# Gate and up products of two transformer layers by Strassen's scheme

## The reference

```
h2 = rmsnorm(x, norm_ffn[l])
gu = einsum('btd,df->btf', h2, w_gate_up[l])      # 1024 x 5632
g, up = split(gu, 2)
x = x + einsum('btf,fd->btd', silu(g) * up, w_down[l])   # 2816 x 1024
```

## Time and profile before

| | |
|---|---|
| median of 3 runs | 2195.66 us (2195.58 to 2195.78) |
| profiled execution | 2195.95 us |
| its span | 2194.1 us |
| busy in the span | PE 2182.2, weight loads 1812.8, DVE 1377.9, ACT 965.4, POOL 74.7 us |
| granted TensorE clock | 0.999 of 2.4 GHz, mean |

### The profile page before, as it was taken

How to read it: one execution, slowest core, us unless ns; L and a number is a source line. 1 busy time by engine, 2 the same in 40 slices (tenths; PEclk the granted TensorE clock), 3 DMA queues, 4 the chain that set the end, 5 groups by cost and what they waited for, 6 DMA issues and landing times.

```text
span 2194.1 us, 28930 instructions
## 1 busy us (share of the span) xinstructions
PE 2182.2 (99%) x10528; PEld 1812.8 (83%) x10528; DVE 1377.9 (63%) x1978; ACT 965.4 (44%) x1392; POOL 74.7 (3%) x103
## 2 busy tenths in 40 slices
PE   9999999999999999999999999999999999999998
PEld 6878888888888878888888888888888899888887
DVE  7999954444345999954444334654776568888723
ACT  5678544443223588544343223332554344333412
POOL 0000020000010000020000010000000000000000
PEclk9999999999999999999999999999999999999999
DMA  5221222222223211222222224223222231222222
GB/s 184 73 80 63 96 96 96 96 96 84 93 93 119 93 62 63 95 96 97 97 99 94 83 92 150 100 81 127 81 97 87 96 135 39 101 99 99 93 96 77
DMA packets 35397, 208.39 MB, mean 95 GB/s; under 512 B 4512, under 2 KB 5024, under 8 KB 14816
## 3 DMA queue, kind: packets, MB, share of 16 engines
q1 hardware_dynamic: 35296, 207.07, 27.2%
HBM read 201.15 MB, written 2.10 MB: 93 GB/s over the span
## 4 chain that ended last, share of the span: by engine, by line
PE 94%; ACT 3%; DVE 2%; issue 1%; DMA 0%; SPq 0%; DVEq 0%; ACTq 0%
PE mm L1796 25%; PE mm L1798 25%; PE mm L1797 25%; PE sp L1798 4%; PE sp L1797 4%; PE sp L1796 4%; PE sp L1898 1%; PE ob L1926 1%; ACT probs L584 1%; DVE conv_y L1171 1%; DVE probs L1201 1%; ACT probs L592 1%; PE sp L1913 0%; PE ob L1798 0%; PE ob L1796 0%
## 5 line engine op out<-in xcount | busy, mean ns | idle before, releaser
L1796 PE MATMUL mm<-in_hi,w_hi 128*128 128x512 f32 (+1 forms) x1696 | 663.6, 391 | 2.9 <-DVE in_lo L1104 2.3
L1798 PE MATMUL mm<-in_hi,w_lo 128*128 128x512 f32 (+1 forms) x1696 | 657.0, 387 | 0.0
L1797 PE MATMUL mm<-in_lo,w_hi 128*128 128x512 f32 (+1 forms) x1696 | 656.9, 387 | 0.0
L525 ACT ACTIVATE w_hi<-w_raw 128x2048 fp32r<-128x2048 f32 (+3 forms) x193 | 346.1, 1794 | 672.7 <-PE mm L1798 562.2
L1070 DVE TENSOR_TENSOR w_lo<-w_raw,w_hi 128x2048 fp32r<-128x2048 f32 (+3 forms) x193 | 422.2, 2188 | 238.7 <-ACT w_hi L525 238.3
L1796 PEld LDWEIGHTS mm<-in_hi,w_hi 128*128 128x128 f32 x1696 | 318.4, 188 | 74.2 <-issue 6.7
L1798 PEld LDWEIGHTS mm<-in_hi,w_lo 128*128 128x128 f32 x1696 | 318.4, 188 | 65.5
L1797 PEld LDWEIGHTS mm<-in_lo,w_hi 128*128 128x128 f32 x1696 | 318.5, 188 | 64.2 <-issue 1.0
L1171 DVE SCALAR_TENSOR_TENSOR conv_y<-conv_in,parl,conv_y 128x512 f32<-128x512 f32 x240 | 169.8, 746 | 1.7
L1081 DVE TENSOR_TENSOR tB<-mm,rstd 128x512 f32<-128x512 f32 x54 | 37.3, 690 | 172.6 <-PE mm L1798 172.6
L1796 PE MATMUL mm<-act_hi,w_hi 128*128 128x512 f32 x352 | 136.9, 389 | 0.0
(11 more groups left out here) (429 smaller groups left out, 3252.9 us busy)
## 6 DMA issues: line engine op xcount, KB each, us to landing
w_raw<-in_w_dram SPq DMA_DIRECT2D x160, 1024.0 KB, 4.8
w_raw<-in_w_dram SPq DMA_DIRECT2D x32, 704.0 KB, 3.9
w_raw<-in_w_dram SPq DMA_DIRECT2D x5, 512.0 KB, 4.5
out_dram<-z_rows SPq DMA_DIRECT2D x8, 256.0 KB, 2.1
rope<-in_rope_dram SPq DMA_DIRECT2D x3, 512.0 KB, 3.9
x<-in_x_dram SPq DMA_DIRECT2D x4, 256.0 KB, 4.9
x<-in_x_dram SPq DMA_DIRECT2D x2, 512.0 KB, 7.6
sq<-ssum SPq DMA_DIRECT2D x32, 32.0 KB, 1.8
```

Source lines behind the costliest of these rows:

```text
L525: e.activation(whi[:, slot, 0:cols], raw[:, slot, 0:cols], ACT.Copy).then_inc(s_whi, whi_out.up())
L1796: MM(out, ah, bh, start=first, stop=False, **kw)
L1797: MM(out, ah, bl, start=False, stop=False, **kw)
L1798: return MM(out, al, bh, start=False, stop=last, **kw)
```

## The change

The gate and up weights of a pair of tiles are seen as a 2 x 2 matrix of blocks: A11 and A12 are the gate tile's first and second four k-tiles, A21 and A22 the up tile's. The tokens are one too: B11, B12, B21, B22, by the first and second four k-tiles and by the first and second 256 tokens. Instead of eight block products, seven are made (Winograd's form of Strassen's scheme), each 4 k-tiles x 3 passes of 256 columns:

- weights: S1 = A21 + A22, S2 = A11 - S1 (the code's wsum 2), S3 = A21 - A11 (wsum 4), S4 = A12 + S2. S1 and wsum 4 are made on POOL (`weight_sums`), the other two on DVE.
- tokens: T1, T2, T3, T4 from differences and sums of the B, made once in a layer by DVE during the output projection.
- products, in TensorE's order for pair p: S1 T1, then A22 T4 of pair p - 1, S2 T2, A12 B21, A11 B11 of pair p + 1, S3 T3, S4 B22. Sums of products are made in PSUM where they can be; three partial results are copied out by ACT (`copied`) and added by DVE (`take_product`).

So the high and low parts of the weights are made in seven pieces of 512 columns (`high_of`, `low_of`), and a raw slot is free once the low part of A22 is made (`load_free`). The chain per pair on DVE is written out in `gated_pair`. The high and low part of the first 12 `act` tiles (`KEPT`) are made only when the stage is over, and the down product takes its k-tiles in the order 12 to 21, 0 to 11 (`DOWN_ORDER`).

The core of the diff, in this order: SP, POOL (`weight_sums`), ACT (to the first `gated_pair`), DVE (to the second), TensorE:

```diff
-L_MM = 102
+L_MM = 58
+KEPT = 12
+DOWN_ORDER = tuple(range(KEPT, FT)) + tuple(range(KEPT))
...
+            def load_free(n, slot, read, cols=CH):
+                e.wait_ge(s_so, read)
+                e.dma_start(raw[:, slot, 0:cols],
+                            W[bass.ds(n, 1), :, 0:cols].rearrange("a p c -> (a p) c")).then_inc(s_raw[slot], 16)
...
+                with L.loop(0, L_GU // 2 - 1) as i:
+                    for c in range(2):
+                        load_free(n + (gate_up + 2) + i * 2 + c, c, operands.now(-8))
+                        operands.skip(7)
...
+                def weight_sums(a, fifth_done):
+                    e.wait_ge(s_raw[a], raws[a].next(16))
+                    e.wait_ge(s_sm, done.now(-fifth_done))
+                    e.tensor_tensor(spot(wsum, 1), raw[:, a, A21], raw[:, a, A22], ALU.add).then_inc(s_su, made.up())
+                    e.wait_ge(s_sm, done.now(-6))
+                    e.tensor_tensor(spot(wsum, 4), raw[:, a, A21], raw[:, a, A11],
+                                    ALU.subtract).then_inc(s_su, made.up())
+                    done.skip(7)
...
+                def next_weights(p):
+                    e.wait_ge(s_su, summed.next())
+                    high_of_sum(1)
+                    e.wait_ge(s_ds, sums.next())
+                    high_of_sum(2)
+                    e.wait_ge(s_sm, done.now(-4))
+                    high_of(3, raw[:, (p + 1) % 2, A12])
+                    e.wait_ge(s_ds, sums.next())
+                    high_of_sum(spot_s4(p + 1))
...
+                def weights_beyond(p):
+                    landed(p % 2)
+                    high_of(0, raw[:, p % 2, A11])
...
+                def gated_pair(p, m, split):
+                    silu()
+                    copied(copy_5[p % 2], bank_z[p % 2], 1)
+                    e.wait_ge(s_su, summed.next())
+                    high_of_sum(4)
+                    e.wait_ge(s_sm, done.now(-2))
+                    high_of(6, raw[:, p % 2, A22])
+                    copied(copy_2[p % 2], bank_x[p % 2], 3)
+                    if split:
+                        act_high(m)
+                    if p < FT - 1:
+                        next_weights(p)
+                        copied(copy_1[(p + 1) % 2], bank_x[(p + 1) % 2], 5)
+                        if p < FT - 2:
+                            weights_beyond(p)
...
+                def out_second(m):
+                    k = m - HK
+                    g_k, g = col(parl, A_GF + k), col(parl, A_GF + m)
+                    t2, t3, t4 = (token_operand(SUM, o, k) for o in (T2, T3, T4))
+                    e.wait_ge(s_fn, fn.next())
+                    STT(t2, t2, g_k, tB[:, 0:TH], ALU.mult, ALU.subtract).then_inc(s_val, val.up())
+                    STT(t3, x[:, k, second_half], g_k, tB[:, 0:TH], ALU.mult, ALU.subtract).then_inc(s_val, val.up())
+                    e.wait_ge(s_val, val.now(1))
+                    STT(t4, x[:, m, first_half], g, t2, ALU.mult, ALU.add).then_inc(s_val, val.up())
+                    token_low(B21, k, x[:, m, first_half], g)
+                    token_low(T2, k, t2)
+                    token_low(T3, k, t3)
+                    token_low(T4, k, t4)
+                    token_low(B22, k, x[:, m, second_half], g)
...
+                def sums_for_next(p):
+                    a = (p + 1) % 2
+                    e.wait_ge(s_su, summed.next())
+                    e.wait_ge(s_sm, done.now(-3))
+                    TT(spot(wsum, 2), raw[:, a, A11], spot(wsum, 1), ALU.subtract).then_inc(s_ds, wsums.up())
+                    low_of_sum(1)
+                    e.wait_ge(s_ds, wsums.now())
+                    TT(spot(wsum, spot_s4(p + 1)), raw[:, a, A12], spot(wsum, 2),
+                       ALU.add).then_inc(s_ds, wsums.up())
...
+                def lows_for_next(p):
+                    low_of_sum(2)
+                    low_of(3, raw[:, (p + 1) % 2, A12])
+                    low_of_sum(spot_s4(p + 1))
...
+                def take_product(dst, bank, other, product, copy):
+                    e.wait_ge(s_sm, done.now(-product))
+                    e.wait_ge(s_sc, copies.now(-copy))
+                    TT(dst, bank, other, ALU.add).then_inc(s_sv, products.up())
...
+                def act_of(p, m, product, told):
+                    e.wait_ge(s_sm, done.now(-product))
+                    e.wait_ge(s_do, own.now())
+                    TT(tile(actf, m, 0, TH), bank_x[p % 2], tC[:, 0:TH], ALU.mult).then_inc(s_sv, products.up())
+                    TT(tile(actf, m, TH, T), tB[:, 0:TH], tC[:, TH:T], ALU.mult).then_inc(told.sem, told.up())
...
+                def lower_takes(p, products_at, beyond):
+                    seventh, third = products_at
+                    take_product(tB[:, 0:TH], bank_x[p % 2], copy_5[p % 2], seventh, 2)
+                    if beyond:
+                        low_of(0, raw[:, p % 2, A11])
+                    take_product(tA[:, TH:T], bank_z[p % 2], copy_2[p % 2], third, 3)
+                    scaled_gate()
...
+                def gated_pair(p, m, split):
+                    scaled_silu()
+                    e.wait_ge(s_su, summed.next())
+                    low_of_sum(4)
+                    act_of(p - 1, m, 2, val if split else own)
+                    low_of(6, raw[:, p % 2, A22])
+                    sums_for_next(p)
+                    if split:
+                        act_low(m)
+                    upper_takes(p, 4)
+                    lows_for_next(p)
+                    lower_takes(p, (6, 7), p < FT - 2)
...
+            def times(out, n, o, start, ready=None):
+                for k in range(HK):
+                    if ready is not None:
+                        e.wait_ge(s_cmb, combos.now(-ready(k)))
+                    a = slice(k * P, k * P + P)
+                    ins = mm3(out, spot(whi, n)[:, a], spot(wlo, n)[:, a], token_operand(HIGH, o, k),
+                              token_operand(LOW, o, k), start and k == 0, k == HK - 1, skip_group_check=True)
+                ins.then_inc(s_sm, done.up())
...
+            def gated_pair(p):
+                a = p % 2
+                e.wait_ge(s_sv, products.now(5))
+                operand(2)
+                times(bank_z[a], 1, T1, True)
+                e.wait_ge(s_sv, products.now(2))
+                operand(1)
+                times(bank_x[1 - a], 6, T4, False)
+                e.wait_ge(s_sc, copies.now(-1))
+                operand(3)
+                times(bank_x[a], 2, T2, False)
+                e.wait_ge(s_sv, products.now(3))
+                operand(4)
+                times(bank_y, 3, B21, True)
+                last = p == FT - 1
+                if not last:
+                    e.wait_ge(s_sv, products.now(0))
+                    operand(6)
+                    times(bank_x[1 - a], 0, B11, True)
+                e.wait_ge(s_sc, copies.now(-3))
+                operand(6 if last else 7)
+                times(bank_x[a], 4, T3, False)
+                e.wait_ge(s_sc, copies.now(-2))
+                operand(5)
+                times(bank_z[a], spot_s4(p), B22, False)
+                if last:
+                    e.wait_ge(s_sv, products.now(-2))
+                    operand(7)
+                    times(bank_x[a], 6, T4, False)
```

More of the change, by code:

```diff
@@ L753, in _ @@
                         prep(m // 4)
[L755 to L765, removed]
@@ L767, in _ @@
+                next_weights(0)
+                copied(copy_1[1], bank_x[1], 5)
+                done.skip(7)
                 e.preload_act_table_set(LN_EXP)
                 e.wait_ge(s_msf, misc_taken.next())
[L769 to L779, removed]
@@ L787, in down @@
+                prep_down(0, 3)
+                e.wait_ge(s_sm, done.now(-4))
+                kept_high(0)
+                kept_high(1)
+                silu()
+                kept_high(2)
+                act_high(FT - 1)
+                prep_down(1, 7)
+                done.skip(7)
+                for m in range(3, KEPT):
+                    kept_high(m)
                 def down(m, d, cols=HALF):
@@ L1377, in _ @@
                         prep((1, 0, 1)[m // 4])
-                def out(m, d):
-                    e.wait_ge(s_mm, tiles.next())
-                    TT(tile(x, m), mm[d][:], tile(x, m), ALU.add).then_inc(s_mmf, taken.up())
-                    in_lo(m, col(parl, m + A_GF))
-                with L.loop(0, L_OUT // 2 - 1) as i:
-                    for c in range(2):
-                        for d in range(2):
-                            out(i * 4 + (2 * c + d), d)
-                        prep(c)
@@ new lines, in _ @@
+                for m in range(HK):
+                    out_first(m)
+                    if m % 2:
+                        prep(m // 2)
+                new_x(HK)
+                out_second(HK)
+                new_x(HK + 1)
+                out_second(HK + 1)
+                low_of(0, raw[:, 0, A11])
```

(23 more changed lines are left out.)

310 lines of the change are left out of this document (270 added, 40 removed).

## The result

The changed kernel took **2241.54 us** (median of 4 runs, 2240.65 to 2242.06); the kernel before took 2195.72 us beside it (2195.58 to 2196.23). The ratio is 1.0207, with a 95% interval of 1.0194 to 1.0219: slower by 46 us, where 2241 had been forecast. The profiled execution took 2241.07 us with a span of 2239.1, against 2194.1 before: 45.0 longer.

A forecast was written before the change was run, and what follows sets the result against it. TensorE bounded the kernel before; DVE with POOL's adds would bound gate and up after. 15 + 12 x 11.5 + 8 x 12.0 + 14 = 263 us against 240.1, +46 over both layers: forecast 2241 us, range 2172 to 2262.

The forecast's parts named there:

- Matmuls: Gate and up pair on TensorE: 84 matmuls of 256 columns at 0.1183 us, 9.94 us instead of 10.88.
- The load ring: Gate and up weight slots, from one low 6 through load, gate, silu and act to the next: period at least 10.9 us.
- DVE with POOL: DVE's work, waits and POOL's adds set the gate and up period: 11.5 us in pairs 1 to 12, 12.0 in 13 to 20.
- 8.3 + 0.8 + 0.3 = 9.4: DVE in pairs 1 to 12: 8.3 us of instructions, 0.8 waiting around silu, 0.3 waiting for low 4's high part.
- the price of an add: Each POOL weight sum in gate and up costs DVE 1.09 us (bounds 0 and 1.35); two a pair, up to 2.2.
- 8.9 + 0.8 + 0.3 = 10.0: DVE from pair 13 on: 8.9 us of instructions including act_low, plus the same waits of 0.8 and 0.3.
- Ends of the stage: Gate and up: first pair 15 us (bounds 11 and 17), including 4.5 of stalls; last pair 14 (10.5 and 15).
- Sum: Gate and up stage: 15 + 12 x 11.5 + 8 x 12.0 + 14 = 263 us against 240.1; +22.8 a layer, +46 in all.
- B: Rival: POOL's adds find gaps, so the load ring alone sets gate and up at 10.9 us a pair; 2206 us, chance 0.25.
- C: Rival: TensorE stays the bound in gate and up, 9.94 us a pair; 2159 us, chance 0.22.
- Its condition: High part of A11 ready by 9.9 us into a pair: load-to-silu ring under 9.94, POOL adds in the gaps.
- D: Rival: DVE's small instructions cost full length, 0.73 not 0.605; gate and up period 13 us, 2294 us, chance 0.08.

The follow-up runs named there:

- Kernel 3: Changed kernel with both POOL sums on 4 columns and gate and up weight loads of 256 columns (output not the reference's): 2173.56 us.
- kernel 1: Changed kernel with both POOL weight sums made on 4 columns instead of 512 (output not the reference's): 2207.73 us.
- kernel 4: Changed kernel with only POOL's first weight sum on 4 columns, the other left whole (output not the reference's): 2213.97 us.
- 8: Changed kernel in its own order, both weight sums of a pair made on DVE, POOL idle: 2210.65 us.
- 5: Changed kernel with ACT's high part of spot 0 (next pair's A11) moved after the silu, DVE's low part after scaling the silu: 2194.11 us.
- 6: Changed kernel with only DVE's low part of spot 0 (next pair's A11) moved after scaling the silu; ACT's order unchanged: 2205.48 us.
- kernel 2: Changed kernel with gate and up weight loads of 256 columns in place of 2048 (output not the reference's): 2221.03 us.
- 7: Changed kernel with the ACT and DVE parts of spot 0 moved later and both POOL sums on 4 columns (output not the reference's): 2173.50 us.
- kernel 10: Changed kernel with 26 matmuls of 256 columns added in the first pair of each layer: 2240.49 us.

## Why the prediction was right, and where only its total was

**Matmuls.** Right: 84 steps of 0.119 us, where 0.118 had been read from the earlier trace rows. Kernel 3 shows what they are worth when all else is out of the way: 9.94 us a pair, the figure of the prediction. In a pair of 11.56 us these steps leave 1.6 us, 14%, and in one of 11.71 15%, as forecast; the windows show 12% and 10% of idle time, since a record is longer than a step.

**The load ring.** Right, at 10.9 us: kernels 1, 4 and 8 lie at 10.82 to 10.86 in pairs 1 to 12 with the load untouched. Its place was right too (low 0 ahead of the last take, kernels 5 and 6).

**DVE with POOL.** The total of 11.5 for pairs 1 to 12 came out at 11.56 by another sum than mine, and that was luck. I had DVE bound by its own chain, 8.3 + 0.8 + 0.3 = 9.4, and by two adds of POOL at 1.09 each. DVE is busy only 81% there, not over 85% (over the whole stage it is 86%), and without the ring it goes at 10.77 (kernel 2), 0.8 under my 11.6. The term that was too large is the price of an add. DVE in kernel 2:

```profile
442.60 0.42 DVE L1694 TENSOR_TENSOR tB<-mm,tB 128x256 f32<-128x256 f32 x1
442.93 1.44 DVE L1610 TENSOR_TENSOR w_lo<-w_raw,w_hi 128x512 fp32r<-128x512 f32 x1
...
444.74 1.32 DVE L1699 TENSOR_TENSOR tA<-tA,rstd 128x512 f32<-128x512 f32 x1
```

Two instructions are stretched from 0.69, by 0.75 and 0.63 us, one by each add: 1.4 in place of 2.2, and 9.4 + 1.4 is the 10.8 measured, so DVE's own 9.4 was right. What was left out is that in the changed kernel the first add lies in the ring: it comes due with the landing of the load, as the ring goes on, and runs beside the one low part that the ring passes through, while the second falls in DVE's wait for the load and costs nothing. So it is ring 10.9 plus a stretch of 0.7, not DVE's sum against the ring's, whichever is longer. Two errors of 0.7 to 0.8 cancelled. In pairs 13 to 20 the forecast's mechanism holds: the short load changes nothing (11.71 both times) and DVE is busy 92% of 480 to 570 us. Without POOL's sums and the long load these pairs take 10.21 (kernel 3), where 8.9 + 0.8 + 0.3 = 10.0 had been added up; the two adds bring 1.50, 0.75 each, where 2.2 had been forecast; so 11.71 stands where 12.0 was.

**How DVE and POOL share.** I took each add to get its turn between two back-to-back instructions of DVE. In the period shown POOL's second sum was ready at 436.25 and lasted 2.69 us, while DVE ran its low parts at their full step of 0.60. The first sum, undisturbed at 439.09, took 1.27; so POOL waited until about 437.7 (an estimate, 436.25 + 2.69 - 1.27), when DVE began a take, which has one operand in PSUM. In pairs 13 to 20 such a take stands earlier, and POOL comes in there and stretches the next low part:

```profile
482.48 1.46 POOL L575 TENSOR_TENSOR w_sum<-w_raw 128x512 f32<-128x512 f32 x1 [7.44 <-PE mm L2180]
482.72 0.42 DVE L1694 TENSOR_TENSOR tA<-sp,tD 128x256 f32<-128x256 f32 x1
483.05 1.44 DVE L1610 TENSOR_TENSOR w_lo<-w_sum,w_hi 128x512 fp32r<-128x512 f32 x1
```

The Trainium skill (SBUF — State Buffer, SBUF: two separate sides) states that a DVE instruction with two SBUF inputs and a GpSimd instruction that reads SBUF hold a shared pair of ports one at a time, whichever starts first, and that the other is blocked. Both places agree with it; which of two queued ones comes first it doesn't say, and at 589.24 POOL did come in between two instructions of DVE that both read SBUF. That stays open.

**Ends of the stage.** Right in sum. Forecast were 15 + 14 = 29 us beside pairs 1 to 20. From the first matmul (316.51) to the first scaling of the gate (336.05) are 19.5 us, the last period has 8.4 and the way to the down product 1.3: 29.3 us before rounding. By TensorE's own matmuls the first pair (84 of them, to 333.26) takes 16.8 us where 15 was forecast, and the last 12.3 where 14 was: the two misses cancel. The remaining periods are 139.9 us (138 forecast) and 92.2 us (96 forecast). The stalls of the first pair are there, 2.1 and 1.1 us, less than the 4.5 that I had given them; some 25 steps at the lower clock, 0.09 us longer each, are most of what the forecast left out.

**Sum.** 261.4 and 263.0 us a layer against 263; +44 and 1 outside, against +46.

**The rivals.** B, the ring alone, is kernel 1: 2207.7 us against the 2206 forecast for it. C, TensorE as the bound, is kernels 3 and 7; 2173.5, not 2159: I had the ends at 23 us a layer and they stay at 28 in kernel 3, whose stage of 229.4 us also has 201.3, not 198.8, for pairs 1 to 20. Its condition was called right: what decides is that the high part of A11 isn't waited for in the gate's chain. D, full length for each small instruction, is out: the low parts step 0.60 (436.52 to 437.12).

## What to carry to other kernels

A transfer that an engine waits for in order belongs behind the work that closes the circle, not ahead of it: moving one high part and one low part by one place was worth 47 us, more than the 40 of TensorE's time that the scheme saves. Work moved to GpSimd is not off VectorE's account: two adds of 512 columns a pair cost 31 us more there than on VectorE itself. When two causes each explain a period, remove each and both, and read each gain as the distance to the next limit: the load came 2.4 us sooner and the pair gained 0.79, since DVE's chain stood behind it; a sum that stretches DVE by 0.75 us showed as 0.07, since the ring stood behind it.

## What was not expected of the hardware

The granted clock fell to 0.50, the 1.2 GHz level, in the first pair of layers 0 and 1, after TensorE had stood for 2.1 us (2.3 in layer 1) and, some 0.9 us of matmuls later, was about to stand for 1.1 (1.0). Some 25 steps of 256 columns then took 0.21 us in place of 0.12. With matmuls in these gaps the clock stayed at 1.00 in the first pair, at no gain in time (kernel 10), and fell in the next. Idle stretches of 1.35 us in every pair didn't bring the clock down (1.00 in both windows of pairs 1 to 20). Nor does the length of one stretch alone tell: after 2.0 us up to 365.03 in kernel 4 it was at 0.50 from 366 to 368 us, and after 3.2 us up to 1051.46 in the changed kernel it stayed at 1.00.
